# Hybrid backbone step on one core: eight modulation blocks move from the mixers to the attention, and the first two weight units are multiplied side by side

## The chip, the cores and the metric

The kernel is one launch on one core of a Trainium2 chip. The metric is device time in microseconds, the median of three runs. The core has five engines that run beside each other and meet at semaphores: TensorE (PE in the rows) for matrix products into PSUM, VectorE (DVE), ScalarE (ACT), GpSimd (POOL), and SyncE (SP), which here issues all the transfers between memory and SBUF. Each engine takes its instructions strictly in the order in which they are written, so an instruction that waits holds back everything behind it on its engine.

## What is computed

One layer of a diffusion backbone over 256 context tokens and 1024 latent tokens of width 1024. The part that matters here, cut from the reference:

```python
def _modulation(cond, w_mod, b_mod):
    m = jax.nn.silu(cond) @ w_mod + b_mod
    return jnp.split(m[:, None, :], N_MOD, axis=-1)      # six parts of 1024 values
...
    shift1, scale1, gate1, shift2, scale2, gate2 = mod
    h = _rmsnorm(x, norm1_g) * (1 + scale1) + shift1
    u = h @ w_in
    q, k, v, p_in, c_in, g_in = _split_in(u)
    y_a = ...attention(q, k, v)...  @ w_oa
    y_b = _pool_mixer(p_in, w_pool, pool_scale) @ w_ob
    y_c = _conv_mixer(c_in, w_dw, b_dw, conv_norm_g, conv_norm_b) @ w_oc
    gates = jax.nn.sigmoid(g_in + b_gate).reshape(B, L, N_BRANCH, D)
    x = x + gate1 * (merged @ w_out)
    h2 = _rmsnorm(x, norm2_g) * (1 + scale2) + shift2
    a, b = jnp.split(h2 @ w_gu, 2, axis=-1)
    x = x + gate2 * ((jax.nn.silu(a) * b) @ w_down)
```

`shift1` and `scale1` are needed at the very start. `gate1`, `shift2` and `scale2` (3072 columns of `w_mod`, 12 blocks of 256 columns, "late" in the kernel) are needed only after the attention, at the residual. There are two condition vectors, one for the latent tokens and one for the context.

## The kernel before

The program has three stages, each with one function per engine: front (`front_engines`, up to about 331 us), attention (`attention_engines`, to about 740 us) and rear (`rear_engines`). Every large product is done in three passes of a split operand, high by high, high by low and low by high (`products`, L143 to L148), so activations exist as `AH` and `AL` and weights as `w_hi` and `w_lo`.

**Front, first tiles.** The 1280 tokens are three chunks (512, 512 and 256 columns), the width is eight tiles of 128. VectorE and ScalarE make `AH` and `AL` tile by tile, in the order of `PAIRS`, eight tiles of chunk 0, eight of chunk 1, eight of chunk 2: `scaled` or the odd branch of `upper`, then `upper` writes `AH` (L677), then `rest` writes `AL` (L903). TensorE starts on weight units 0 and 1 while tiles still come. `unit_chunk(0, 0)` waits for each tile as it is made (L415 to L418); `unit_chunk(1, 0)` then goes over the same eight tiles again; then `spread_rstd(2)` (L538), whose result the normalisation of chunk 2 waits for; then units 0 and 1 on chunk 1, and on chunk 2, the first one waiting for tiles again. Products go to a ring of four PSUM banks (`RING`, `JOBS`): a bank is taken again when the job four before it has been read, by ScalarE or by VectorE (`glu_out`, L827).

**Front, the late modulation.** A block of 256 columns is loaded whole (1 MB, `load_mod`, L295), VectorE multiplies its eight row tiles by the two condition vectors into an accumulator (`modulation`, two instructions at L816 and fourteen at L819), and TensorE sums the accumulator over partitions with a column of ones (`modulation`, L431, four products written, eight in the records). All twelve blocks are made so, at the places of `MOD_AT` on TensorE and at the places written out in `vector`: six between 84 and 128 us, six between 259 and 317 us. Between them VectorE runs the 31 taps of the convolution (L839). `late_mod` adds the bias at the end of the front.

**Attention.** Eight heads of ten steps, 80 steps `s`, with `h = s // 10` and `n = s % 10`; steps 0 to 7 of a head are latent queries, 8 and 9 the context's. In step `s` TensorE does the scores of `s` (L1281 against the local keys, L1287 against the past ones), the transposes of step `s - 2` (L1296), and the products with V of step `s - 3` (L1310). Between them it does pieces of the gate projections (`gate_piece`, L147), spread evenly, which need nothing of the softmax. VectorE in its step `s` does: the maximum of the scores (`maximum`, L1440, L1443, L1445), the sum and reciprocal of `s - 1` (`total`, L1453, L1455), the sum of V products (`gather`, L1475), the low part of the transposed probabilities of `s - 2` (`lower`, L1462), and then in some steps more: `prepare` at `n == 5` (L1424) and `add_rows` at `n` 3 and 4 (L1481). ScalarE does the exponentials (L1361 past, L1364 local), the high part of the transposed probabilities (L1373), and between them gate rows (L1354) and splits of weights (L1333), keys (L1339), queries (L1342) and values (L1345). GpSimd normalises the probabilities (L1528), and makes the low parts of weights, keys and values and the bias tables (L1503, L1509, L1512, L1522).

The scores of step `s` use one pair of banks, so TensorE waits for ScalarE's exponential of the past scores of `s - 1` before it writes the next ones:

```python
                if s:
                    pe.wait_ge(past_ready, s)
```

and that exponential waits for VectorE's maximum of `s - 1`. This is the tightest tie between TensorE and VectorE in the stage.

**SyncE in the attention** walks the same steps: gate rows out, keys of the next head at `n == 0`, half of the position bias at `n` 1 and 2 (`load_b`, eight small transfers each, L1194), queries at 3, values at 6, weights between them (L1173).

## Time and profile before

| what | value |
|---|---|
| median of 3 runs | 1858.1 us (1857.86 to 1858.96) |
| the profiled execution: device time | 1857.35 us |
| the profiled execution: span of the instructions | 1855.5 us |
| TensorE busy | 1834.8 us, 99% |
| VectorE, ScalarE, GpSimd busy | 60%, 40%, 27% |
| granted clock of TensorE | 0.999 over the span |

The profile is one execution. Busy time is the union of an engine's instructions; TensorE's matmuls are pipelined, so they overlap in the records and the real cost of one is the distance from its start to the next one's start. A bracket behind a row tells how long the engine was idle before it and whose work ended that idle time. A row with no bracket followed at once on the one before it on its engine (gaps under about 0.15 us carry none).

### The profile page before, as it was taken

How to read it: one execution, taken by the hardware profiler on the slowest of the kernel's cores; microseconds unless marked ns; L12 is line 12 of the kernel's file. 1: busy time of each engine (PE TensorE's matmuls, PEld its weight loads, DVE VectorE, ACT ScalarE, POOL GpSimd, SP SyncE). 2: the span in 40 equal slices, each digit the busy share in tenths (PEclk: the TensorE clock that was granted, in tenths of full speed). 3: DMA queues.
4: the chain of work that ended last, by engine and by line, in shares of the span. 5: the costliest groups of instructions: out<-in, count | busy, mean ns of one | idle time of the engine just before them, and what ended most of it. 6: DMA issues, size and time to landing. Idle time of an engine off the chain costs nothing.

```text
span 1855.5 us, 26797 instructions
## 1 busy us (share of the span) xinstructions
PE 1834.8 (99%) x10034; PEld 1574.7 (85%) x10034; DVE 1115.5 (60%) x2090; ACT 748.4 (40%) x1412; POOL 500.5 (27%) x378
## 2 busy tenths in 40 slices
PE   8999999999999999999999999999999999999998
PEld 3788888898888888888888888888888888888898
DVE  4799997155655554276217755555444444799984
ACT  5612232355555554444224522222222223445474
POOL 0000000344444432144542243444434441000000
PEclk9999999999999999999999999999999999999999
DMA  8471345443344332765531222232122224866665
GB/s 329 160 225 48 113 130 190 114 133 104 101 111 113 104 99 67 240 186 173 189 125 46 97 69 91 97 97 67 54 74 74 74 74 169 280 210 222 210 215 199
DMA packets 221057, 253.91 MB, mean 137 GB/s; under 512 B 32384, under 2 KB 159872, under 8 KB 219904
## 3 DMA queue, kind: packets, MB, share of 16 engines
q1 hardware_dynamic: 220928, 252.20, 42.8%
q8 instruction: 80, 1.31, 0.3%
q14 instruction: 49, 0.40, 0.1%
HBM read 191.60 MB, written 60.56 MB: 136 GB/s over the span
## 4 chain that ended last, share of the span: by engine, by line
PE 95%; DVE 1%; DMA 1%; ACT 1%; issue 1%; POOL 0%; SPq 0%; ACTq 0%; DVEq 0%
PE ps_all L147 72%; PE ps_all L2425 5%; PE ps_all L2426 5%; PE ps_all L2427 4%; PE ps_all L1310 2%; PE ps_all L1296 2%; PE ps_all L1281 1%; PE ps_all L1287 1%; PE ps_all L527 1%; DMA wmod_block<-w_mod_dram 1%; PE ps_all L431 1%; DVE Y L3080 0%; PE ps_all L2459 0%; DMA wmod_then_mixers<-w_mod_dram 0%; PE ps_all L453 0%
## 5 line engine op out<-in xcount | busy, mean ns | idle before, releaser
L147 PE MATMUL ps_all<-AH,w_hi 128*128 128x512 f32 (+1 forms) x1376 | 493.4, 359 | 1.9 <-ACT gate_rows L1354 1.0
L147 PE MATMUL ps_all<-AH,w_lo 128*128 128x512 f32 (+1 forms) x1376 | 483.6, 351 | 0.0
L147 PE MATMUL ps_all<-AL,w_hi 128*128 128x512 f32 (+1 forms) x1376 | 483.1, 351 | 0.0
L147 PEld LDWEIGHTS ps_all<-AH,w_lo 128*128 128x128 f32 x1376 | 259.8, 189 | 35.9
L147 PEld LDWEIGHTS ps_all<-AH,w_hi 128*128 128x128 f32 x1376 | 260.2, 189 | 33.8 <-DVE AL L903 1.9
L147 PEld LDWEIGHTS ps_all<-AL,w_hi 128*128 128x128 f32 x1376 | 260.4, 189 | 30.3
L2999 DVE TENSOR_TENSOR quarter<-ps_all,quarter 128x512 f32<-128x512 f32 x140 | 96.6, 690 | 177.9 <-PE ps_all L147 175.8
L2852 POOL TENSOR_TENSOR slot_lo<-w_pair,slot_hi 128x512 fp32r<-128x512 f32 x96 | 129.8, 1376 | 174.1 <-ACT slot_hi L2623 174.1
L147 PE MATMUL ps_all<-AH,slot_hi 128*128 128x256 f32 (+1 forms) x384 | 129.5, 337 | 0.0
L147 PE MATMUL ps_all<-AL,slot_hi 128*128 128x256 f32 (+1 forms) x384 | 129.2, 336 | 0.0
L147 PE MATMUL ps_all<-AH,slot_lo 128*128 128x256 f32 (+1 forms) x384 | 129.1, 336 | 0.0
L2852 POOL TENSOR_TENSOR w_lo<-w_pair,w_hi 128x512 fp32r<-128x512 f32 x64 | 85.4, 1354 | 114.4 <-ACT w_hi L2623 114.4
L1462 DVE TENSOR_TENSOR PT<-ps_all,PT 128x256 fp32r<-128x256 f32 (+1 forms) x144 | 61.6, 465 | 83.6 <-ACT PT L1373 83.6
L1528 POOL TENSOR_SCALAR prob<-prob,softmax_cols 128x640 f32<-128x640 f32 (+2 forms) x80 | 57.5, 719 | 167.5 <-DVE softmax_cols L1455 167.2
L1361 ACT ACTIVATE prob<-ps_all,softmax_cols 128x256 f32<-128x256 f32 x80 | 38.0, 475 | 130.5 <-DVE softmax_cols L1445 113.5
L839 DVE SCALAR_TENSOR_TENSOR xT_then_mixers<-wmod_then_mixers,cols,xT_then_mixers 128x1295 f32<-128x1295 f32 x60 | 89.5, 1591 | 0.0
L2425 PE MATMUL ps_all<-AH 128*128 128x512 f32 (+1 forms) x248 | 86.9, 350 | 1.1 <-DVE AL L3035 1.1
L2427 PE MATMUL ps_all<-AH,AL 128*128 128x512 f32 (+1 forms) x248 | 86.3, 348 | 0.0
L2426 PE MATMUL ps_all<-AL,AH 128*128 128x512 f32 (+1 forms) x248 | 86.3, 348 | 0.0
L2425 PE MATMUL ps_all<-AH,w_hi 128*128 128x512 f32 (+1 forms) x236 | 83.9, 355 | 0.0
L2427 PE MATMUL ps_all<-AH,w_lo 128*128 128x512 f32 (+1 forms) x236 | 83.3, 353 | 0.0
L2426 PE MATMUL ps_all<-AL,w_hi 128*128 128x512 f32 (+1 forms) x236 | 83.3, 353 | 0.0
(307 smaller groups left out, 3948.8 us busy)
## 6 DMA issues: line engine op xcount, KB each, us to landing
w_raw<-w_in_dram SPq DMA_DIRECT2D x42, 512.0 KB
w_pair<-w_gu_dram SPq DMA_DIRECT2D x20, 1024.0 KB, 5.1
hidden_in<-hidden SPq DMA_DIRECT2D x77, 256.0 KB, 3.0
wmod_then_mixers<-w_mod_dram SPq DMA_DIRECT2D x19, 1024.0 KB, 8.1
hidden<-quarter SPq DMA_DIRECT2D x50, 256.0 KB, 2.1
branch_and_gates<-gates SPq DMA_DIRECT2D x16, 768.0 KB, 4.4
w_down_rows<-w_down_dram SPq DMA_DIRECT2D x44, 256.0 KB, 3.4
gates<-gate_rows SPq DMA_DIRECT2D x42, 256.0 KB, 2.2
```

What stands on the lines that cost most here:

```text
L147: mm = nc.tensor.matmul(out, w, a[:, k, cols[0]:cols[1]], start=(first and part == 0), stop=(last and part == 2))
L839: nc.vector.scalar_tensor_tensor(conv[:, t, :], glu[:, t, k:k + CV], w, conv[:, t, :], ALU.mult, ALU.add).then_inc(conv_step, 1)
L1296: mm = nc.tensor.transpose(psT[:, turned_at(j):turned_at(j) + P], prob[:, s % 3, j * P:(j + 1) * P], g.ident[:, :])
L1310: mm = nc.tensor.matmul(psV[s % 2][:, 0:2 * P], VV[:, b, v, :], PT[:, s % 2, j, :], start=(m == 0), stop=(m == len(both) - 1))
L1361: nc.scalar.activation(pr[:, LOCAL:PCOLS], psS_past, ACT.Exp, bias=c[:, 2:3], accum_out=c[:, 4:5]).then_inc(past_ready, 1)
L1462: nc.vector.tensor_tensor(PT[:, s % 2, j0:j1, P:2 * P], psT[:, turned_at(j0):turned_at(j0) + (j1 - j0) * P].rearrange("p (j n) -> p j n", ...
L1528: nc.gpsimd.tensor_scalar(pr[:, a:PCOLS], pr[:, a:PCOLS], c[:, 5:6], 1.0, ALU.mult, ALU.mult).then_inc(normal, 1)
L2425: nc.tensor.matmul(out, wh, th, start=first, stop=False)
L2426: nc.tensor.matmul(out, wh, tl, start=False, stop=False)
L2427: return nc.tensor.matmul(out, wl, th, start=False, stop=last)
L2852: nc.gpsimd.tensor_tensor(tiles4(lo), in_pair(p, idx), tiles4(hi.bitcast(F32)), ALU.subtract).then_inc(s_lo, 1)
L2999: nc.vector.tensor_tensor(temp[TEMP[out][side]][:, :], g.ps_all[:, product_bank(p, source), :], temp[TEMP[first][side]][:, :], ALU.add).th ...
```

## The change

Two edits.

1. Four of the twelve late blocks stay in the front, at new places of `MOD_AT`. The other eight are made in the attention, one per head: SyncE loads 1 MB into a single buffer `late_wmod` at step `n == 1`, VectorE does the sixteen instructions in groups of 2, 2, 2, 2, 3, 3, 2 at the ends of its steps `n` = 3 to 9 (`MOD_OPS`), and TensorE sums them at step `n == 2` of the next head. The copy from PSUM and `late_mod` move to the end of the attention. The semaphores of the modulation become shared over the stages, and the rear's `gate2` counts on from them.
2. Units 0 and 1 are multiplied side by side in `first_units`, so that each tile is used by both units when it comes; in chunk 1 the first four tiles are still taken by unit 0 alone and then by unit 1 alone, the last four by both.

```diff
-MOD_AT = {(2, 2): (0,), (3, 0): (1,), (3, 1): (2,), (4, 0): (3,), (4, 1): (4,), (5, 0): (5,), (13, 2): (6,),
-          (14, 0): (7,), (15, 0): (8,), (15, 1): (9,), (16, 1): (10,), (17, 0): (11,)}
+MOD_STEPS = 2 * KD
+MOD_ALL, MOD_FRONT = 3 * D // (2 * P), 4
+MOD_AT = {(3, 0): (0,), (3, 2): (1,), (4, 1): (2,), (5, 0): (3,)}
+MOD_OPS = {3: (0, 2), 4: (2, 4), 5: (4, 6), 6: (6, 8), 7: (8, 11), 8: (11, 14), 9: (14, 16)}
...
+            def first_units(c):
+
+                a, b = CHUNKS[c]
+                pe.wait_ge(W.lo_ready, 2)
+                out = {}
+                alone = 4 if c == 1 else 0
+                for k, units in [(k, (u,)) for u in range(2) for k in range(alone)] + [(k, (0, 1)) for k in range(alone, KD)]:
+                    w = slice(k * P, (k + 1) * P)
+                    pe.wait_ge(ah_ready, c * KD + k + 1)
+                    for u in units:
+                        if k == 0:
+                            out[u] = bank(JOB["unit", u, c])[:, 0:b - a]
+                        hi, lo = w_slot(u)
+                        nc.tensor.matmul(out[u], hi[:, w], g.AH[:, k, a:b], start=(k == 0), stop=False)
+                        nc.tensor.matmul(out[u], lo[:, w], g.AH[:, k, a:b], start=False, stop=False)
+                    pe.wait_ge(al_ready, c * KD + k + 1)
+                    for u in units:
+                        mm = nc.tensor.matmul(out[u], w_slot(u)[0][:, w], g.AL[:, k, a:b], start=False, stop=(k == KD - 1))
...
-            unit_chunk(0, 0)
-            unit_chunk(1, 0)
+            first_units(0)
             spread_rstd(2)
-            for c in (1, 2):
-                for u in range(2):
-                    unit_chunk(u, c)
+            first_units(1)
+            first_units(2)
...
             lower(4)
-            modulation(3)
-            modulation(4)
             for c in range(3):
                 glu_out(1, c)
             lower(5)
-            modulation(5)
+            modulation(3)
...
             lower(14)
-            modulation(6)
-            modulation(7)
             normalise()
-            lower(15)
-            modulation(8)
-            modulation(9)
-            lower(16)
-            modulation(10)
-            lower(17)
-            modulation(11)
-            lower(18)
-            late_mod()
+            for u in range(15, 19):
+                lower(u)
...
+            def load_mod(n):
+                if n > MOD_FRONT:
+                    sp.wait_ge(acc_step, MOD_STEPS * n)
+                sp.dma_start(late_w[:, :, :], g.d["w_mod"].rearrange("(k p) n -> p k n", p=P)[:, :, 2 * D + n * 2 * P:2 * D + (n + 1) * 2 * P]).then_inc(mod_in, 16)
...
+                if n == 1 and h < MOD_ALL - MOD_FRONT:
+                    load_mod(MOD_FRONT + h)
...
+                if s % QT == 2 and s > QT:
+                    pe.wait_ge(summed_v, s - TIMES - 1)
+                    modulation(MOD_FRONT + s // QT - 1)
...
+            def modulation(n, first, last):
+                if first == 0:
+                    dve.wait_ge(mod_in, 16 * (MOD_FRONT // 2 + n - MOD_FRONT + 1))
+                    dve.wait_ge(mod_used, n)
+                for at in range(first, last):
+                    k, j = at // 2, at % 2
+                    w, c, acc = late_w[:, k, :], g.cs[:, at:at + 1], late_acc[:, j, :]
+                    if k == 0:
+                        nc.vector.tensor_scalar(acc, w, c, None, ALU.mult).then_inc(acc_step, 1)
+                    else:
+                        dve.wait_ge(acc_step, MOD_STEPS * n + at - 1)
+                        nc.vector.scalar_tensor_tensor(acc, w, c, acc, ALU.mult, ALU.add).then_inc(acc_step, 1)
...
+                if n in MOD_OPS and h < MOD_ALL - MOD_FRONT:
+                    modulation(MOD_FRONT + h, *MOD_OPS[n])
             add_rows(HEADS - 1, 1)
+            late_mod()
```

TensorE, units 0 and 1 on chunk 0. Before, unit 0's last tile and then the start of unit 1 over the same tiles:

```order
L415 MATMUL ps_all<-AH,w_hi 128x512 [waits ah_ready]
L416 MATMUL ps_all<-AH,w_lo 128x512
L418 MATMUL ps_all<-AL,w_hi 128x512 [waits al_ready]
L147 MATMUL ps_all<-AH,w_hi 128x512 [waits w_lo_ready]
L147 MATMUL ps_all<-AL,w_hi 128x512
L147 MATMUL ps_all<-AH,w_lo 128x512
```

After, one tile:

```order
L425 MATMUL ps_all<-AH,w_hi 128x512 [waits ah_ready]
L426 MATMUL ps_all<-AH,w_lo 128x512
L425 MATMUL ps_all<-AH,w_hi 128x512
L426 MATMUL ps_all<-AH,w_lo 128x512
L429 MATMUL ps_all<-AL,w_hi 128x512 [waits al_ready]
L429 MATMUL ps_all<-AL,w_hi 128x512
```

Each wait for a tile has six products behind it in place of three, and the pass of unit 1 over chunk 0 that waited for nothing is gone.

VectorE, the end of step 4 of head 0 and the start of step 5 in the attention. Before:

```order
L1475 TENSOR_REDUCE OT<-ps_all 128x16x8 [waits times_v]
L1462 TENSOR_TENSOR PT<-ps_all,PT 128x3x128 [waits p_hi0]
L1462 TENSOR_TENSOR PT<-ps_all,PT 128x2x128 [waits p_hi1]
L1440 ISA prob,softmax_cols<-ps_all,bias 128x384 [waits t_done1,local_scored]
L1443 TENSOR_REDUCE softmax_cols<-ps_all 128x1 [waits scored]
```

After, from the end of step 3 of the same head to the same place:

```order
L1498 TENSOR_SCALAR late_mod_acc<-late_wmod,silu_c 128x256 [waits mod_acc_used,late_wmod_in0]
L1498 TENSOR_SCALAR late_mod_acc<-late_wmod,silu_c 128x256
L1447 ISA prob,softmax_cols<-ps_all,bias 128x384 [waits t_done1,local_scored]
...
L1469 TENSOR_TENSOR PT<-ps_all,PT 128x3x128 [waits p_hi0]
L1469 TENSOR_TENSOR PT<-ps_all,PT 128x2x128 [waits p_hi1]
L1501 SCALAR_TENSOR_TENSOR late_mod_acc<-late_wmod,silu_c,late_mod_acc 128x256 [waits mod_acc_step] x2
L1447 ISA prob,softmax_cols<-ps_all,bias 128x384 [waits t_done1,local_scored]
```

The new instructions stand between the low part of one step and the maximum of the next; the first of a head waits for the block's transfer.

SyncE, step 1 of head 0. Before:

```order
L1179 DMA kq_src<-kT_dram 64x1536 [waits v_lo]
L1179 DMA kq_src<-kT_dram 64x1536
L1194 DMA bias_src<-rpb_dram 8x8x24 [waits bias_ready]
L1194 DMA bias_src<-rpb_dram 8x8x24 x7
L1207 DMA gates<-gate_rows 128x512 [waits gate_free]
```

After:

```order
L1166 DMA kq_src<-kT_dram 64x1536 [waits v_lo]
L1166 DMA kq_src<-kT_dram 64x1536
L1181 DMA bias_src<-rpb_dram 8x8x24 [waits bias_ready]
L1181 DMA bias_src<-rpb_dram 8x8x24 x7
L1204 DMA late_wmod<-w_mod_dram 128x8x256
L1194 DMA gates<-gate_rows 128x512 [waits gate_free]
```

The block's load stands behind the keys and the first half of the bias, and ahead of the next gate rows.

## Rows read from the trace of the kernel before

**Rows 1.** Table by stretch, the attention (columns: stretch, its length, busy per engine, clock).

```profile
350.00:740.00 390.00, 388.98 (x2376) 345.43 (x2375) 213.74 (x662) 217.49 (x551) 158.34 (x130) 1.00 0.38 104
```

**Rows 2.** The chain that ended last, in order of time: start us, us, what.

```profile
165.25 5.46 PE ps_all L147 x24
170.93 8.35 PE ps_all L147 x48
```

**Rows 3.** TensorE in order of time, first units: start us, us, engine, line, instruction.

```profile
49.56 0.47 PE L415 MATMUL ps_all<-AH,w_hi 128*128 128x512 f32 x1 [1.03 <-ACT AH L677]
...
59.18 0.50 PE L418 MATMUL ps_all<-AL,w_hi 128*128 128x512 f32 x1 [0.70 <-DVE AL L903]
...
71.39 0.50 PE L147 MATMUL ps_all<-AH,w_hi 128*128 128x512 f32 x1 [0.62 <-DVE AL L903]
...
83.41 1.04 PE L482 MATMUL ps_all<-ident,vt 128*128 128x128 f32 x8
```

**Rows 4.** VectorE in order of time beside them: tiles of AL, and the first `glu_out`.

```profile
64.15 0.69 DVE L903 TENSOR_TENSOR AL<-normed,AH 128x512 fp32r<-128x512 f32 x1
...
70.65 0.69 DVE L903 TENSOR_TENSOR AL<-normed,AH 128x512 fp32r<-128x512 f32 x1
...
74.70 0.68 DVE L827 TENSOR_TENSOR wmod_then_mixers<-ps_all,sig 128x512 f32<-128x512 f32 x1
```

**Rows 5.** TensorE in order of time, one block of the late modulation and what follows.

```profile
98.07 0.95 PE L431 MATMUL ps_all<-ones,mod_acc 128*128 128x1 f32 x8
98.88 0.48 PE L147 MATMUL ps_all<-AH,w_hi 128*128 128x512 f32 x1
```

**Rows 6.** VectorE, one block of the late modulation, in order of time.

```profile
83.95 0.61 DVE L816 TENSOR_SCALAR mod_acc<-wmod_then_mixers,silu_c 128x256 f32<-128x256 f32 x2
84.48 5.63 DVE L819 SCALAR_TENSOR_TENSOR mod_acc<-wmod_then_mixers,silu_c,mod_acc 128x256 f32<-128x256 f32 x14
```

**Rows 7.** View of the buffer `wmod_then_mixers`, 80 to 340 us: its transfers' landing.

```profile
DMA to landing us min/median/max: 5.1/7.0/10.1
```

**Rows 8.** Waits in the attention: who, for whom, us in total, times, longest.

```profile
DVE prob L1440 <- PE ps_all L1281: 52.1, 37, 4.0
```

**Rows 9.** VectorE, head 1: start of the maximum in steps 5 to 7.

```profile
428.21 0.54 DVE L1440 CUSTOM_DVE_ANT_0 prob<-ps_all,bias 128x384 f32<-128x384 f32 x1
...
433.91 0.56 DVE L1440 CUSTOM_DVE_ANT_0 prob<-ps_all,bias 128x384 f32<-128x384 f32 x1
...
437.48 0.42 DVE L1440 CUSTOM_DVE_ANT_0 prob<-ps_all,bias 128x256 f32<-128x256 f32 x1
```

**Rows 10.** ScalarE, then TensorE: head 1, past scores of step 6 read, step 7 written.

```profile
435.10 0.47 ACT L1361 ACTIVATE prob<-ps_all,softmax_cols 128x256 f32<-128x256 f32 x1 [2.74 <-DVE softmax_cols L1445]
...
436.88 0.28 PE L1287 MATMUL ps_all<-KA,QS 128*128 128x256 f32 x1
```

**Rows 11.** The same two in head 5, steps 6 and 7.

```profile
621.19 0.48 ACT L1361 ACTIVATE prob<-ps_all,softmax_cols 128x256 f32<-128x256 f32 x1 [2.53 <-DVE softmax_cols L1445]
...
622.00 0.28 PE L1287 MATMUL ps_all<-KA,QS 128*128 128x256 f32 x1
```

**Rows 12.** GpSimd, then VectorE, in head 1: the low keys and a one-column sum.

```profile
413.59 3.51 POOL L1509 TENSOR_TENSOR KB<-kq_src,KA 128x1536 fp32r<-128x1536 f32 x1 [1.87 <-ACT KA L1339]
...
414.75 2.36 DVE L1453 TENSOR_TENSOR softmax_cols<-softmax_cols 128x1 f32<-128x1 f32 x1
```

**Rows 13.** VectorE by shape, 1060 to 1300 us: one addition, two sources (xcount, busy, mean ns).

```profile
L3012 DVE SCALAR_TENSOR_TENSOR quarter<-quarter,quarter 128x512 f32<-128x512 f32 x17 | 19.0, 1136 | 1.0
...
L3012 DVE SCALAR_TENSOR_TENSOR quarter<-ps_all,quarter 128x512 f32<-128x512 f32 x4 | 2.7, 681 | 0.0
```

**Rows 14.** SyncE, VectorE and TensorE in head 0, steps 1 to 5.

```profile
370.75 2.93 SPq L1194 DMA_DIRECT2D bias_src<-rpb_dram  x8
...
375.88 0.55 DVE L1440 CUSTOM_DVE_ANT_0 prob<-ps_all,bias 128x384 f32<-128x384 f32 x1
...
380.32 0.28 PE L1287 MATMUL ps_all<-KA,QS 128*128 128x256 f32 x1
```

More of the change, by code:

```diff
@@ L412, in unit_chunk @@
                     w = slice(k * P, (k + 1) * P)
-                    if u == 0 and c == 0:
-                        pe.wait_ge(ah_ready, k + 1)
-                        nc.tensor.matmul(out[:, 0:b - a], hi[:, w], g.AH[:, k, a:b], start=(k == 0), stop=False)
-                        nc.tensor.matmul(out[:, 0:b - a], lo[:, w], g.AH[:, k, a:b], start=False, stop=False)
-                        pe.wait_ge(al_ready, k + 1)
-                        mm = nc.tensor.matmul(out[:, 0:b - a], hi[:, w], g.AL[:, k, a:b], start=False, stop=(k == KD - 1))
-                        continue
-                    if u == 0:
-                        pe.wait_ge(al_ready, c * KD + k + 1)
                     mm = products(nc, out[:, 0:b - a], hi[:, w], lo[:, w], g.AH, g.AL, k, (a, b), k == 0, k == KD - 1)
                 mm.then_inc(done, 1)
+            def first_units(c):
[15 more added lines that the diff above has]
+                        mm = nc.tensor.matmul(out[u], w_slot(u)[0][:, w], g.AL[:, k, a:b], start=False, stop=(k == KD - 1))
+                        if k == KD - 1:
+                            mm.then_inc(done, 1)
             def modulation(n):
@@ L1023, in gpsimd @@
             nc.gpsimd.tensor_tensor(sig[:, :], sig[:, :], square, ALU.add).then_inc(sq_summed, 1)
-        return Engines(sync, tensor, scalar, vector, gpsimd, ((mod_step, 2), (branch_stored, 16 * 6)), after, signals)
+        return Engines(sync, tensor, scalar, vector, gpsimd, ((W.lo_ready, MIX + 1), (branch_stored, 16 * 6)), after, signals)
 V_PARTS = ((0, 4), (4, 8), (8, 10))
@@ L1121, in attention_engines @@
         st = sb("softmax_cols", [P, 4, 6])
+        late_w = nc.alloc_sbuf_tensor_at("late_wmod", [P, KD, 2 * P], F32, offset=aligned(nc.sbuf_base))
+        late_acc = nc.alloc_sbuf_tensor_at("late_mod_acc", [P, 2, 2 * P], F32, offset=aligned(nc.sbuf_base) + 4 * KD * 2 * P)
+        mod_in, acc_step, mod_used, mod_out, mod_step = g.mod_in[0], g.acc_step, g.mod_used, g.mod_out, g.mod_step
         psG = g.ps_all[:, 0:2, :]
@@ L1311, in value, with modulation @@
                 mm.then_inc(times_v, 1)
+            def modulation(n):
+                pe.wait_ge(acc_step, MOD_STEPS * (n + 1))
+                for m in range(2):
+                    for j in range(2):
+                        c = 4 * n + 2 * m + j
+                        mm = nc.tensor.matmul(g.modp[:, c:c + 1], late_acc[:, j, m * P:(m + 1) * P], g.ones[:, 0:1], start=True, stop=True)
+                mm.then_inc(mod_used, 1)
             for x in range(LEAD):
@@ L1481, in add_rows, with late_mod @@
                 nc.vector.tensor_tensor(rows, rows, OLO[:, 0:b - a], ALU.add).then_inc(out_ready, 1)
+            def modulation(n, first, last):
[10 more added lines that the diff above has]
+                        nc.vector.scalar_tensor_tensor(acc, w, c, acc, ALU.mult, ALU.add).then_inc(acc_step, 1)
+            def late_mod():
+                dve.wait_ge(mod_out, 1)
+                mod = g.mod[:, 2 * KD:5 * KD, :]
+                nc.vector.tensor_tensor(mod, mod, g.cols[:, OFF["b_mod"] + 2 * KD:OFF["b_mod"] + 5 * KD].rearrange("p (m j) -> p m j", j=1).broadcast_to([P, 3 * KD, 2]),
+                                        ALU.add).then_inc(mod_step, 1)
+                dve.wait_ge(mod_step, 1)
+                mod_gain(g, 1, "norm2_g", 4, mod_step)
             prepare(0)
```

57 lines of the change are left out of this document (24 added, 33 removed).

## The prediction

> **What bounds the kernel now.** I read four views, in this order. The table by stretch first: over the attention TensorE is busy 389.0 of 390 us, VectorE 213.7, GpSimd 158.3 [rows 1]. So the time is TensorE's work plus the few places where it stands, and whatever is put on VectorE is free just as long as TensorE does not come to wait for it. The chain gives the price of that work: 24 products of 512 columns take 5.46 us, 0.2275 us each, and 24 of 512 with 24 of 256 take 8.35 us, so one of 256 costs 0.120 us [rows 2]. TensorE's own timeline then shows where it stands: from the first product of unit 0 at 49.56 us to the transposes of the cached keys at 83.41 us it needed 33.85 us [rows 3] for 96 products of 512 columns (21.84 us) and 48 of 256 (5.76 us), 27.6 us in all. About 6.2 us of this stretch is waiting for tiles, and TensorE has no other such hole. Last, the waits inside the attention, to see how far VectorE is from being late there.
>
> **Part 1, the first units.** Nothing is added or removed, only the order changes. The walk, with tiles counted 1 to 24 over the three chunks. Chunk 0: both units take 1.365 us per tile; the last AL tile of the chunk comes at 59.1 (the product that waited for it starts at 59.18 [rows 3]), the pace of TensorE is slower than that of the tiles, so it runs 48 products without standing, 49.56 + 10.92 = 60.5. Before, unit 1 ended at about 65.0. Chunk 1: unit 0 alone meets tile 12, whose AL ends at 64.15 + 0.69 = 64.84 [rows 4], so its fourth tile is done at 65.1; unit 1 alone takes 2.73, to 67.9; the last four tiles for both take 5.46, to 73.3, the last tile being there since 71.34 [rows 4]. Before, both ended at about 77.7. Chunk 2: unit 1's bank is free only when VectorE has read job (1, 0), an instruction at 74.70 that ends at 75.38 [rows 4] and stands behind tile work in VectorE's order; since the spread for chunk 2 comes earlier, it may move up by 0.6. TensorE gets the bank at about 74.9 and needs 0.24 less than 5.76 from there: 80.4. Against 83.41 that is **3.0 us gained**, half of the hole. The other half is held by the making of tiles and by that bank. It can't be more than 6.2 (no hole left) or less than 0 unless the later bank wait grows by 3 us, for which no row speaks.
>
> **Part 2, the eight blocks leave the front.** On TensorE one block costs 98.88 - 98.07 = 0.81 us [rows 5]. Eight are taken out of the front and eight put into the attention: 0 in the sum. On VectorE one block costs 0.53 for its first two instructions and 5.63 for the other fourteen, 0.40 each [rows 6], 6.1 us together. Taking them out of the front buys nothing by itself, since TensorE waits for no VectorE work between 85 and 331 us; it gives cover, so that VectorE keeps ahead of a TensorE that now comes 3 us sooner. The transfers are the same eight megabytes.
>
> **Part 3, the eight blocks in the attention.** Of the 64 maxima of the latent steps only 37 waited for TensorE's scores [rows 8]; the other 27 started when VectorE had finished its previous step. In those steps VectorE and ScalarE are one serial chain: maximum, exponential, high part, low part, then rows or queries, then the next maximum. In head 1 the maxima of steps 5, 6 and 7 start at 428.21, 433.91 and 437.48 with no idle time before them [rows 9]. The new instructions stand exactly there, between low part and maximum, so each is added whole to the chain. TensorE notices when ScalarE's exponential of the past scores comes too late. In head 1 that of step 6 ends at 435.57 and TensorE's next past scores start at 436.88 [rows 10], their weight load about 0.1 before, so 1.2 us are to spare; the delay by then is 0.6 + 0.8 + 0.8 = 2.2 us, less the 0.8 by which TensorE's own block at step 2 puts it later. In head 5 the same pair stands at 621.67 and 622.00 [rows 11], 0.2 to spare, and 1.65 arrives. I carried the delay from step to step through all heads in this way, adding 0.6, 0.8, 0.8, 0.8, 1.2, 1.2 and 0.8 at steps 3 to 9, taking off what VectorE idled before a maximum, and counting what goes beyond the room before each step's past scores: 0.0, 0.6, 0.3, 0.7, 0.3, 1.4, 0.0 and 1.1 us for heads 0 to 7, **4.5 us lost**. If the delay is a fifth smaller, the same walk gives about 1.4, if a fifth larger, about 8.
>
> To this come two things that the count of instructions doesn't have. **The port.** While GpSimd ran the low keys from 413.59 to 417.10, VectorE's one-column addition of 0.15 us, started at 414.75, ended at 417.11 [rows 12]. Of the 64 such additions ten took over 0.3 us, and each of the ten ended within 0.03 us of a GpSimd instruction with two sources in SBUF. Fourteen of a block's sixteen instructions read two sources in SBUF, and GpSimd does its weights, tables and values in steps 6 to 8, after VectorE's sum of the same step, so they meet. In the rear an addition with both sources in SBUF took 1136 ns mean beside GpSimd, 681 ns with one source in PSUM [rows 13], 1.67 times. By that ratio the ten instructions of steps 6 to 9 cost 4.0 x 0.67 = 2.7 us more per head, 21 us in all; some is taken up by VectorE's idle time in steps 9 to 2. Ends: 0 if they never meet, and 22 by the same walk if every meeting that today's order shows is paid in full. I take a third, **7.5 us**. The Trainium skill states the mechanism (SBUF — State Buffer, Who interferes with whom): a VectorE instruction with two SBUF inputs and a GpSimd instruction that reads SBUF block each other for the whole instruction, whichever starts first. The trace agrees with it in the ten cases; taken for every meeting it would make the sum some 14 us larger than mine, which is the upper end above.
>
> **The transfer in head 0.** SyncE's last bias transfer of step 1 is issued by 373.68, the block's load right behind it; the maximum of step 4, before which VectorE now takes the block's first two instructions, started at 375.88 [rows 14]. The same load landed in 5.1, 7.0 and 10.1 us (least, median, most) in the front [rows 7], so it comes at 378.8 to 383.8. VectorE stands for 3 to 8 us. TensorE's past scores of step 5 at 380.32 [rows 14] have 2.6 us of room, and the chain of steps 5 to 7 is full. With a wait of 4.2 the walk gives 4.1 us, with 3 it gives 2.9, with 8 it gives 7.9. I take **4 us**. In the other heads step 3 comes some 10 us after the load's issue, and it is there.
>
> **The sum.** -3.0 + 4.5 + 7.5 + 4.0 = +13.0 us. On the profiled execution's 1857.35 that is 1870.4; it lies 0.75 under the median, so on the median it is 1871.1. The end of the attention (copy and bias, below 1 us on ScalarE and VectorE) is hidden: both stand idle for over 5 us there, and the bank that waits for the copy is the last of eight.
>
> **The rivals.**
> *Covered.* VectorE has 176 us idle in the attention [rows 1] and the 49 us fit in. TensorE never waits beyond a microsecond or two, and the 3.0 stay: 1855.1, up to 1858 with part of head 0's wait. For it speaks that no PE wait on VectorE shows in the stage; against it rows 9 to 11, where room is 0.2 and 1.2 us.
> *Faster, by the whole hole.* The tiles of chunk 1 and 2 come sooner than in my walk, since TensorE's earlier spread frees VectorE and the bank read moves up, and all 6.2 us go: 1858.1 - 6.2 = 1851.9, if the attention is covered too. It decides whether AL's 16th tile is made before about 70. Against it: VectorE shows no idle time between 56 and 65 us.
> *Transfers.* The megabyte per head also delays weights and gate rows that are queued behind it, and ScalarE stands for them in order. In head 5 weights are issued right behind it. It adds 1 to 5 us per head where it hits: 1885 and over.
>
> **How the numbers follow.** Chances: the forecast (VectorE's chain gets too long in the attention, port and first transfer with it) 0.62, own range 1862 to 1885; covered 0.2; the whole hole 0.08; transfers 0.1. The most likely time is that of the forecast, 1871. The range reaches down to the covered case, 1855, and up to 1886, where head 0 waits the longest and the port costs double. A measurement of this kernel can tell about 0.2%, 3.7 us, from no change. Faster by more than that: the whole hole and a little of the covered case, 0.13. Within it: most of the covered case and the mildest end of the forecast, 0.22. Slower: 0.65.
>
> **What would show it.** Right: TensorE reaches the cached keys' transposes 2.5 to 3.5 us earlier; the front ends about 9.5 us earlier; in the attention TensorE waits at the scores (now L1270 to L1281) for ScalarE, most in head 0 and in steps 6 to 9; the attention is longer by 6.5 us of products plus 10 to 22 us of standing; the new products' partner on VectorE, L1501, has a mean over 0.5 us with single ones over 1 us; L1498 waits for `late_wmod` in head 0. Wrong: VectorE's steps 3 to 7 keep their length, which would mean that the chain had room that I took for none; or L1501 keeps 0.48 us throughout, and the port term is 0; or the first block's load lands before 376.

## The result

The changed kernel takes 1872.24 us (median, 1871.31 to 1872.58) against 1857.86 (1857.66 to 1858.96): ratio 1.0075, 95% interval 1.0066 to 1.0085. The prediction was 1871.1, slower. Its profiled execution has a span of 1870.3 us, 14.8 more than before.

The span, cut at TensorE's own marks (its first product of unit 0, the transposes of the cached keys, the first scores, the last product with V), says where:

| stretch | before | after | difference | predicted |
|---|---|---|---|---|
| start to first product | 49.56 | 49.78 | +0.2 | 0 |
| first units | 33.85 | 30.82 | -3.0 | -3.0 |
| rest of the front | 275.18 | 267.54 | -7.6 | -6.5 |
| attention | 380.61 | 406.34 | +25.7 | +22.5 |
| rear | 1116.3 | 1115.8 | -0.5 | 0 |

Of the attention's 25.7, 7.2 are the eight blocks' products. The prediction took 0.81 a block [rows 5], but the first product behind a block also starts its successor 0.09 late, so a block is 0.90, here as in the front, and moving it cancels. The other 18.5 are time in which TensorE stands or runs at half clock; 16.0 had been predicted.

The table by stretch of the changed kernel, the attention, answers to [rows 1] (stretch, length, busy per engine, clock):

```profile
350.00:740.00 390.00, 380.13 (x2294) 334.73 (x2293) 275.69 (x774) 205.05 (x535) 153.79 (x126) 0.99 0.44 119
```

TensorE is now busy 380.1 of 390, and VectorE 275.7 instead of 213.7. That is 62 us more in a stretch where 49 had been counted. VectorE still stands idle for 114 us here, and the work costs TensorE 18 us all the same.

The first units, in order of time, answer to [rows 3] and [rows 4] (start us, us, engine, line, instruction, in brackets the idle time and who ended it):

```profile
49.78 0.47 PE L425 MATMUL ps_all<-AH,w_hi 128*128 128x512 f32 x1 [1.02 <-ACT AH L683]
...
73.74 0.28 PE L426 MATMUL ps_all<-AH,w_lo 128*128 128x256 f32 x1
74.98 0.39 PE L425 MATMUL ps_all<-AH,w_hi 128*128 128x256 f32 x1 [0.97 <-DVE wmod_then_mixers L830]
...
80.60 1.04 PE L490 MATMUL ps_all<-ident,vt 128*128 128x128 f32 x8
```

49.78 to 80.60 is 30.82; the last wait is for the bank that `glu_out` reads, as the walk had it: 74.98 and 80.60 against 74.9 and 80.4.

The groups of instructions over the attention (xcount, busy us, mean ns, idle before) and two waits (who, for whom, us in total, times, longest):

```profile
L1501 DVE SCALAR_TENSOR_TENSOR late_mod_acc<-late_wmod,silu_c,late_mod_acc 128x256 f32<-128x256 f32 x112 | 69.9, 670 | 0.1
...
L1498 DVE TENSOR_SCALAR late_mod_acc<-late_wmod,silu_c 128x256 f32<-128x256 f32 x16 | 5.9, 409 | 4.4 <-DMA late_wmod<-w_mod_dram 4.4
```

```profile
PE ps_all L1281 <- ACT prob L1366: 5.8, 9, 1.4
...
PE ps_all L1275 <- DVE softmax_cols L1447: 2.4, 1, 2.4
```

The accumulations have a mean of 0.67 us. The view of their tile gives the least as 0.469, the middle as 0.477 and the longest as 2.619: most are as short as in the front, and 22 of 112 took 0.6 to 2.6. Each of the 22 started while a GpSimd instruction ran and ends 0.27 to 0.28 us behind its end. Nine of the 90 short ones overlap one too; there it was GpSimd that started later. The costliest piece in head 2:

```profile
488.71 3.41 DVE L1501 SCALAR_TENSOR_TENSOR late_mod_acc<-late_wmod,silu_c,late_mod_acc 128x256 f32<-128x256 f32 x3
489.18 2.66 POOL L1534 TENSOR_TENSOR w_lo<-w_raw,w_hi 128x1024 fp32r<-128x1024 f32 x1 [1.61 <-ACT w_hi L1338]
```

Three accumulations take 3.41 us instead of 1.2, since the third ends only when GpSimd's low part of the weights has ended at 491.84.

The last large piece is head 0. TensorE in order of time (rows between are left out where the dots stand), then the table by stretch beside it (the eighth column, behind GpSimd's, is the granted clock):

```profile
368.93 0.75 PE L1304 MATMUL ps_all<-PT,VV 128*128 128x256 f32 x5
372.11 0.69 PE L1275 MATMUL ps_all<-KA,QS 128*128 128x384 f32 x1 [2.43 <-DVE softmax_cols L1447]
...
374.31 0.63 PE L149 MATMUL ps_all<-AL,w_hi 128*128 128x512 f32 x1
374.74 0.63 PE L149 MATMUL ps_all<-AH,w_lo 128*128 128x512 f32 x1
```

```profile
366.00:369.00 3.00, 3.00 (x19) 2.62 (x19) 0.00 (x0) 1.49 (x1) 1.30 (x1) 1.00 1.06 353
...
374.00:376.00 2.00, 2.00 (x6) 1.53 (x6) 1.75 (x5) 0.85 (x3) 0.00 (x0) 0.50 0.74 193
...
378.00:380.00 2.00, 2.00 (x9) 1.60 (x8) 0.89 (x2) 2.00 (x6) 0.27 (x2) 0.79 0.01 4
```

VectorE stood 4.4 us for the first block's load (the eight loads land, by the view of their buffer, 5.2 to 6.0 us after the issue), TensorE 2.4 for VectorE. Not all of this is the load. VectorE's first two instructions behind it, and GpSimd beside them:

```profile
369.87 1.70 DVE L1498 TENSOR_SCALAR late_mod_acc<-late_wmod,silu_c 128x256 f32<-128x256 f32 x2 [4.37 <-DMA late_wmod<-w_mod_dram]
367.70 3.46 POOL L1540 TENSOR_TENSOR KB<-kq_src,KA 128x1536 fp32r<-128x1536 f32 x1 [3.59 <-ACT KA L1344]
```

The two take 1.70 us instead of the 0.61 of [rows 6]: the late load put the first of them beside GpSimd's low keys, and 1.1 us of the wait are this meeting. When TensorE went on, a product of 512 columns took 0.43 us instead of 0.23, until 378.9: the granted clock was 0.50, that is 1.2 GHz. The 6.7 us at half clock did the work of 3.4, so 3.3 us were lost on top of the 2.4. No step of the prediction had that.

### The profile page after: what moved, and what is told of

The parts are those of the page before. It is cut to its first block, busy times and chain, and to the rows that moved or that the text cites. A ratio compares the mean times of both kernels' runs of the same rounds, so it can differ in the third digit from the quotient of the medians.

```text
span 1870.3 us, 26800 instructions
## 1 busy us (share of the span) xinstructions
PE 1841.1 (98%) x10034; PEld 1579.4 (84%) x10034; DVE 1136.1 (61%) x2090; ACT 745.3 (40%) x1412; POOL 502.9 (27%) x378
## 4 chain that ended last, share of the span: by engine, by line
PE 83%; DVE 6%; ACT 4%; issue 3%; DMA 2%; POOL 1%; SPq 0%; ACTq 0%; DVEq 0%; POOLq 0%
PE ps_all L149 63%; PE ps_all L2457 4%; PE ps_all L2459 4%; PE ps_all L2458 4%; DVE late_mod_acc L1501 2%; PE ps_all L1304 1%; PE ps_all L1290 1%; ACT PT L1378 1%; PE ps_all L535 1%; DMA wmod_block<-w_mod_dram 1%; DVE prob L1447 1%; ACT prob L1369 1%; DVE PT L1469 1%; PE ps_all L1281 1%; PE ps_all L1275 1%
## 5 line engine op out<-in xcount | busy, mean ns | idle before, releaser
L149 PE MATMUL ps_all<-AH,w_hi 128*128 128x512 f32 (+1 forms) x1336 | 479.5, 359 | 0.7 <-ACT gate_rows L1359 0.5
L149 PE MATMUL ps_all<-AH,w_lo 128*128 128x512 f32 (+1 forms) x1336 | 470.3, 352 | 0.0
L149 PE MATMUL ps_all<-AL,w_hi 128*128 128x512 f32 (+1 forms) x1336 | 470.0, 352 | 0.0
L149 PEld LDWEIGHTS ps_all<-AH,w_lo 128*128 128x128 f32 x1336 | 252.7, 189 | 35.0
L149 PEld LDWEIGHTS ps_all<-AH,w_hi 128*128 128x128 f32 x1336 | 253.2, 190 | 31.1 <-ACT gate_rows L1359 1.0
L149 PEld LDWEIGHTS ps_all<-AL,w_hi 128*128 128x128 f32 x1336 | 253.3, 190 | 29.7
L2457 PE MATMUL ps_all<-AH,w_hi 128*128 128x512 f32 (+1 forms) x236 | 83.9, 355 | 0.0
L2459 PE MATMUL ps_all<-AH,w_lo 128*128 128x512 f32 (+1 forms) x236 | 83.3, 353 | 0.0
L2458 PE MATMUL ps_all<-AL,w_hi 128*128 128x512 f32 (+1 forms) x236 | 83.3, 353 | 0.0
```

What stands on the lines that cost most here:

```text
L149: mm = nc.tensor.matmul(out, w, a[:, k, cols[0]:cols[1]], start=(first and part == 0), stop=(last and part == 2))
L2457: nc.tensor.matmul(out, wh, th, start=first, stop=False)
L2458: nc.tensor.matmul(out, wh, tl, start=False, stop=False)
L2459: return nc.tensor.matmul(out, wl, th, start=False, stop=last)
```

## The experiments

The walk through the attention had three terms: the chain's length 4.5, the port 7.5, the first load 4.0. The accounts to be told apart were that transfers do it, that the port (GpSimd holding up VectorE) costs nothing on the path, and that the two parts of the change are independent of each other. The times of the kernel before beside these runs were 1858.0 to 1858.5 us (median).

**1. The first units alone** (the kernel before with `first_units`):

```diff
-            unit_chunk(0, 0)
-            unit_chunk(1, 0)
+            first_units(0)
             spread_rstd(2)
-            for c in (1, 2):
-                for u in range(2):
-                    unit_chunk(u, c)
+            first_units(1)
+            first_units(2)
```

> The kernel before with the new order of the first two units and nothing else; all twelve blocks stay beside the mixers. My theory, that the two parts are independent: TensorE is 3.0 us earlier at the transposes of the cached keys and keeps it to the end, 1857.9 - 3.0 = 1854.9. Rival, that the gain needs the blocks out of the front (VectorE must keep ahead of a TensorE that comes sooner): the 3.0 us are given back by waits before 331 us, 1857.9.

**2. The blocks alone** (the changed kernel with those lines as before):

> The changed kernel with the first two units in the old order. If the parts are independent, it loses the 3.0 us and stands at 1872.2 + 3.0 = 1875.2. If the new order only moved waits about, it stands at 1872.2.

Measured: alone, the first units bring nothing, 1858.86 us, ratio 1.0001 (0.9991 to 1.0010). The blocks alone take 1875.0 (1.009, 1.0075 to 1.0105), 2.8 over the changed kernel. So the new order is worth 2.8 with four blocks in the front and nothing with twelve. In run 1 TensorE was at the transposes after 30.83 us, as in the changed kernel, and lost the gain again from 118.8 us on. VectorE and TensorE there, and the table by stretch:

```profile
114.93 5.62 DVE L829 SCALAR_TENSOR_TENSOR mod_acc<-wmod_then_mixers,silu_c,mod_acc 128x256 f32<-128x256 f32 x14
...
120.48 1.61 DVE L837 TENSOR_TENSOR wmod_then_mixers<-ps_all,sig 128x512 f32<-128x512 f32 x3
...
121.21 0.80 PE L147 MATMUL ps_all<-AH,w_hi 128*128 128x512 f32 x1 [2.38 <-DVE wmod_then_mixers L837]
```

```profile
121.00:124.30 3.30, 3.09 (x7) 2.48 (x8) 3.30 (x8) 0.00 (x0) 0.00 (x0) 0.50 0.80 247
```

TensorE waits for a bank that `glu_out` has to read, and `glu_out` stands behind the fourteen accumulations of block 4. Again it stands 2.4 us, and again the clock is at half behind it, to 124.4. The kernel before came to this place at 121.0 us, when the read that it needs, begun at 119.7, was done, and had neither.

**3. The first load before step 0, and 5, in step 0.** The block is loaded ahead of the loop of steps, or behind the weights of unit 3:

```diff
             load_v(0)
+            load_mod(MOD_FRONT)          # run 3
             for s in range(STEPS_END + 1):
...
                 if s == 0:
                     load_w(3)
+                    load_mod(MOD_FRONT)  # run 5
...
-                if n == 1 and h < MOD_ALL - MOD_FRONT:
+                if n == 1 and 0 < h < MOD_ALL - MOD_FRONT:
```

> The changed kernel with one transfer moved: the first block of the attention is loaded before step 0 instead of in step 1. In the changed kernel head 0 is longer than before by 5.65 us beyond its block's 0.81, the others by 1.1 to 2.8, 1.9 in the mean. My theory: VectorE's wait for the load holds up TensorE, which stands and is then granted half its clock for some 6.7 us; both go, 3.8 us, 1868.4, and no stretch of half clock is left. Rival, the half clock has nothing to do with the wait: the clock falls all the same, and about half of the 3.8 stays, 1870.3.

Measured: 1871.29 (1.0071, 1.0056 to 1.0086), a miss. The half clock is gone and head 0 is 1.4 us shorter, not 3.8. ScalarE's row in head 0 says why:

```profile
357.50 1.06 ACT L1339 ACTIVATE w_hi<-w_raw 128x1024 fp32r<-128x1024 f32 x1 [4.60 <-DMA w_raw<-w_in_dram]
```

The megabyte now ran ahead of the weights of unit 3, ScalarE stood 4.6 us for those, with the exponentials behind it in its order. This is the prediction's transfer rival, made by the experiment and not by the change.

> The changed kernel with the first block's load in step 0 right behind the weights of unit 3 (before step 0 it pushed those weights back and ScalarE stood 4.6 us for them). My theory, that head 0 lost 3.8 us to the wait for the load and to the half clock that followed it: head 0 goes from 51.5 to 47.8 us and the kernel to 1868.4. Rival, whatever place the megabyte has, it pushes some other transfer back, and head 0 stays at about 50: 1871.

Measured: 1868.94 (1.0055, 1.0040 to 1.0070), head 0 is 48.04 us instead of 51.53, the attention 402.56 instead of 406.34. The first load's place is worth 3.8 us of the attention (3.3 by the two medians, which were taken beside different runs of the kernel before). Runs 6, 7, 9 and 10 build on this one.

**4. One source instead of two** (on run 3; the adding up is left out):

```diff
-                        nc.vector.scalar_tensor_tensor(acc, w, c, acc, ALU.mult, ALU.add).then_inc(acc_step, 1)
+                        at0 = min(k * 2 * P, KD * 2 * P - ONE_WIDE)
+                        nc.vector.tensor_scalar(acc, late_w.ap().rearrange("p k n -> p (k n)")[:, at0:at0 + ONE_WIDE], c, None, ALU.mult).then_inc(acc_step, 1)
```

> As the run before, and the fourteen accumulations of a block in the attention are replaced by products with one source in SBUF, of 314 columns instead of 256 so that one takes the same 0.40 us; the adding up is left out, so the modulation of those columns is not computed. Same count, same place, same time of one. If the shared port is what made 22 of the 112 take 0.64 to 2.6 us, none of them does now, VectorE's share is 45 us instead of 70, and only my term for the lengthened chain is left: 1854.9 + 4.5 = 1859.4. Rival, the long ones cost nothing on the path and the chain's own length is what TensorE waits for: 1868.

Measured: 1864.62 (1.0034, 1.0021 to 1.0047), between the two. It does not test what it was made for. The view of the tile:

```profile
L1504 DVE TENSOR_SCALAR late_mod_acc<-late_wmod,silu_c x112: 366/376/2512, 372.5 to 734.3; 128x314 f32<-128x314 f32 x112
```

25 of the 112 are long again, up to 2.5 us. And they were not of equal length: from start to start one took 0.29 us, not 0.40. The gain of 6.7 us over run 3 is put down to the shorter instructions, which this run doesn't show by itself; what it does show is that one source in SBUF does not avoid GpSimd.

**6 and 10. Reductions** (on run 5), over 384 and over 320 columns:

```diff
-                        nc.vector.scalar_tensor_tensor(acc, w, c, acc, ALU.mult, ALU.add).then_inc(acc_step, 1)
+                        at0 = min(k * 2 * P, KD * 2 * P - ONE_WIDE)
+                        nc.vector.tensor_reduce(acc[:, at:at + 1], late_w.ap().rearrange("p k n -> p (k n)")[:, at0:at0 + ONE_WIDE], AX, ALU.add).then_inc(acc_step, 1)
```

> As the run before, and each of the fourteen accumulations is replaced by a reduction over 384 columns of the same block: one source in SBUF, one column written, an estimated 0.40 us each. The modulation of these columns is left out. In the run with products of one source 24 of 112 were still long, so the number of sources does not decide. Theory A, any VectorE instruction with a source in SBUF meets GpSimd: again some 20 long ones, VectorE's share about 70 us, and the kernel at 1868. Theory B, the reduction does not take the port: no long ones, share 45 us, and the standing in heads 1 to 7 falls to my chain term, 1860.

> The reductions again over 320 columns instead of 384. With 384 one took 0.46 us from start to start, not the 0.40 of an accumulation; with 320 it should take 0.39. So this is the chain's length at the right size with no meeting. By the walk of the prediction, 4.5 us at this length, on the 1854.5 of the run that keeps two of sixteen: 1859.0. Rival, the standing does not fall so steeply with the length: over 1861.

Measured: 1863.19 with 384 columns (1.0026, 1.0016 to 1.0035) and 1860.49 with 320 (1.0015, 1.0005 to 1.0025). No reduction is long. The view of the tile with 320, and then the same place in head 1, step 6, first of the changed kernel, then with reductions:

```profile
L1504 DVE TENSOR_REDUCE late_mod_acc<-late_wmod x112: 466/475/488, 370.5 to 730.2; 128x1 f32<-128x320 f32 x112
```

```profile
434.58 2.38 POOL L1534 TENSOR_TENSOR w_lo<-w_raw,w_hi 128x1024 fp32r<-128x1024 f32 x1
...
435.88 1.76 DVE L1501 SCALAR_TENSOR_TENSOR late_mod_acc<-late_wmod,silu_c,late_mod_acc 128x256 f32<-128x256 f32 x2
```

```profile
430.24 2.38 POOL L1537 TENSOR_TENSOR w_lo<-w_raw,w_hi 128x1024 fp32r<-128x1024 f32 x1
...
431.53 0.87 DVE L1504 TENSOR_REDUCE late_mod_acc<-late_wmod 128x1 f32<-128x320 f32 x2
```

GpSimd runs the same instruction over the same moment; two accumulations take 1.76 us, two reductions 0.87, which is their time alone. With 320 columns a reduction is as long as an accumulation alone (middle 0.475 and 0.477), in the same count and place. So this pair, runs 5 and 10, differs by the meetings only: attention 402.56 and 393.87, **8.7 us**. Theory B of run 6 holds. The tables by stretch of run 5, run 10 and, for what follows, run 7 (TensorE's busy time is the first number behind the length, VectorE's the third):

```profile
350.00:735.00 385.00, 376.40 (x2286) 331.35 (x2286) 272.89 (x770) 205.37 (x534) 154.08 (x125) 1.00 0.44 120
...
350.00:735.00 385.00, 381.92 (x2332) 337.95 (x2331) 254.50 (x782) 209.60 (x541) 154.86 (x128) 1.00 0.44 121
...
350.00:735.00 385.00, 384.65 (x2371) 342.52 (x2370) 213.41 (x672) 211.90 (x543) 154.95 (x128) 1.00 0.45 124
```

The meetings are 18 us of VectorE's time, and TensorE loses about half of that.

**7. Two of sixteen** (on run 5):

```diff
-                for at in range(first, last):
+                for at in range(first, min(last, 2)):
...
-                        nc.vector.tensor_scalar(acc, w, c, None, ALU.mult).then_inc(acc_step, 1)
+                        nc.vector.tensor_scalar(acc, w, c, None, ALU.mult).then_inc(acc_step, MOD_STEPS // 2)
```

> As the load in step 0, with only the first two of a block's sixteen instructions left on VectorE (fourteen left out, so the modulation of these columns is not computed); all loads and all of TensorE's products stay. My theory, that transfers cost nothing by themselves in heads 1 to 7: attention as long as before plus 8 x 0.9 for the products, 380.6 + 7.2 = 387.8, and the kernel at 1855 to 1856. Rival, the loads hold up weights and gate rows: 1 us or more per head, 1862 or over.

Measured: 1854.47 (0.9979, 0.9969 to 0.9988), attention 388.26, 0.5 over before plus the products, all of it in head 0. Eight megabytes and eight blocks of products cost nothing more; the transfer rival is out for heads 1 to 7. From here to run 10 only VectorE's work grows, by 41 us (254.50 against 213.41): 393.87 - 388.26 = **5.6 us**, the chain's length by itself.

**9. Ahead of the low part** (on run 5): the call of `modulation` is moved in front of `lower(s - TURN)`.

```diff
+                if n in MOD_OPS and h < MOD_ALL - MOD_FRONT:
+                    modulation(MOD_FRONT + h, *MOD_OPS[n])
                 if 0 <= s - TURN < STEPS:
                     lower(s - TURN)
...
-                if n in MOD_OPS and h < MOD_ALL - MOD_FRONT:
-                    modulation(MOD_FRONT + h, *MOD_OPS[n])
```

> As the load in step 0 (1868.9), and in a step the block's instructions stand ahead of VectorE's low part of the probabilities instead of behind it. There VectorE waits for ScalarE's high part, 69 us in 74 waits, 0.93 each, and two instructions take 0.8. Theory, the price is the place in the chain: the part that is only length (with reductions, which never meet GpSimd, 8 of the 14 us of standing) goes, what the meetings cost stays: 1861. Rival, the chain is a sum wherever the instructions stand: 1868.9.

Measured: 1865.25 (1.0039, 1.0024 to 1.0054), attention 399.35: 3.2 us better, not 8. The view of the tile and a wait:

```profile
L1502 DVE SCALAR_TENSOR_TENSOR late_mod_acc<-late_wmod,silu_c,late_mod_acc x112: 468/827/2627, 368.2 to 733.4; 128x256 f32<-128x256 f32 x112
```

```profile
PE ps_all L1291 <- DVE PT L1470: 6.5, 7, 1.6
```

In the new place the accumulations meet GpSimd's normalising of the probabilities: 70 of 112 are long, 45 of these end just behind a normalising, and the middle one of all takes 0.83 us. TensorE now stands for the low part that comes behind them. The gap in VectorE's order was real, but it is the gap in which GpSimd works.

**8, 11 and 12. All twelve blocks in the front, with the new order of the first units.** In run 8 the products of the second gate unit stand ahead of block 4:

```diff
             modulation(3)
-            modulation(4)
             for c in range(3):
                 glu_out(1, c)
+            modulation(4)
             lower(5)
```

> The kernel before with the new order of the first units, and in VectorE's order the three products of the second gate unit (L827) stand ahead of block 4 instead of behind it; all twelve blocks in the front. In the run with the first units alone TensorE stood 2.4 us at 118.6 for the first of these three, which waited behind block 4, and was then granted half its clock to 124.4; that ate the gain. If that is all, the 3.0 us come through: 1855.4. If the next wait in line takes its place: 1858.

Measured: 1856.64 (0.9989, 0.9980 to 0.9998). The stand at 118.8 is gone, and 1.8 of the 3.0 arrive, against the 1858.45 of the kernel before beside it (the 1.3 in what was expected of run 11 counts from 1857.9). The waits of the front name the next in line:

```profile
PEld ps_all L147 <- DVE w_lo L815: 1.3, 2, 1.0
PEld ps_all L147 <- ACT gate_rows L1364: 1.3, 1, 1.3
```

They are the low parts of weights that VectorE makes between the taps of the convolution, at 200 and 216 us, and gate rows at 353.

Run 11 takes block 5 behind the convolution as well, and the bias to the end of the attention; run 12 also puts a low part between any two of the last three. VectorE's order, run 8 against run 12 (in run 11 blocks 9 and 10 stand together ahead of `lower(17)`; the places on TensorE and of the loads, which follow this order and are the same in runs 11 and 12, are left out):

```diff
             lower(5)
-            modulation(5)
...
             lower(14)
+            modulation(5)
             modulation(6)
-            modulation(7)
             normalise()
             lower(15)
+            modulation(7)
             modulation(8)
-            modulation(9)
             lower(16)
-            modulation(10)
+            modulation(9)
             lower(17)
-            modulation(11)
+            modulation(10)
             lower(18)
+            modulation(11)
-            late_mod()
```

> All twelve blocks in the front again, new order of the first units, the second gate unit's products ahead of block 4, and block 5 moved from before the convolution to behind it (seven late blocks instead of six); the bias of the modulation is added at the end of the attention. VectorE enters the convolution 6 us sooner. With the gate products first the kernel was at 1856.6: 1.3 of the 3.0 us came through, since TensorE then waited 0.3 and 0.9 us at 200 and 216 us for the low parts of weights which VectorE makes between taps. Theory, VectorE is the second limit of the front and this gives it room: 1855.2. Rival, the longer late part holds TensorE up between 265 and 330 us: 1857 or over.

> As the run with seven late blocks, but behind the convolution every block stands between two low parts of weights on VectorE (block 9, low part of unit 17, block 10, low part of unit 18, block 11); the attention's first transfers wait for the last block. With blocks 9 and 10 in one piece TensorE stood 3.7 us at 311 for the low part of unit 17 and 1.9 at 358.8 for gate rows, whose place in ScalarE's order is behind keys that came 4.5 us later. Theory, VectorE's order is all that stood in the way, the whole 3.0 us come through: 1855.2, or 1855.6 with a little of the end. Rival, the second limit of the front is VectorE's total work and another low part comes late: 1857 or over.

Measured: run 11 takes 1862.43 (1.0023, 1.0013 to 1.0033), run 12 takes 1854.33 (0.9980, 0.9971 to 0.9989), faster than both kernels of this study. In run 11 most is one wait of TensorE, for a low part behind two blocks, with half clock to 318 behind it:

```profile
PE ps_all L150 <- DVE w_lo L809: 3.7, 1, 3.7
```

A second stand, 1.9 us at 356.9 for gate rows, has half clock behind it too. Run 12 has no wait of TensorE for VectorE between 82 us and the attention, and its VectorE does the same work there, so the amount of work was not the limit. That VectorE's order alone is worth the 8.1 us between runs 11 and 12 is not shown: run 12 also lets the attention's first transfers go at the last block instead of the last low part, and which of the two removed the stand for gate rows is open.

## Why the prediction came out right, and where it did not

**First units, -3.0:** measured -3.03. The walk over tiles, and the bank behind job (1, 0), hold to 0.2 us. But runs 1 and 2 show that this term was not the property of the edit: with twelve blocks in the front and VectorE's order as it was, it is worth nothing. The sentence that TensorE waits for no VectorE work between 85 and 331 us was read from the old trace and holds for the old TensorE. Part 2 named the cover that the moved blocks give and priced it at nothing; beside the old order of VectorE it is the whole 3.0, and run 12 shows that the cover can be had without moving a block, by another order.

**Chain, 4.5:** measured 5.6 (runs 7 and 10). The walk from step to step, with 0.2 to 3 us of room before each step's past scores [rows 10, 11], is good to a fifth in the sum. (The eight numbers that it lists add up to 4.4.) By head it is less good, and part of the agreement is luck: it gave 0.0, 0.6, 0.3, 0.7, 0.3, 1.4, 0.0 and 1.1 us for heads 0 to 7, and run 10 is longer than run 7 by 1.0, 1.5, 0.3, 0.7, 1.0, 1.1, 0.0 and 0.0. The walk also had the steepness: with instructions a sixth longer (run 6) the attention is 3.8 us longer, but 2.0 of these are in head 0, where TensorE stood 1.4 for ScalarE, which had itself waited 4.4 us for weights; 1.8 are in the other heads. VectorE has over 100 us idle at the same time; by the share of busy time, the covered rival, it should have cost nothing.

**Port, 7.5:** measured 8.7 (runs 5 and 10), inside 0 to 22. That it came near the third that I had taken is luck: the prediction had rows for the two ends and none for the third. The ratio under it was misread as well: of the 17 additions of [rows 13] five ran beside no GpSimd instruction and took 0.69, the other twelve took 1.0 to 1.8. The reason given was also incomplete. The count of sources does not decide: products with one source met GpSimd as often (run 4), reductions with one source never (runs 6, 10). The Trainium skill has what I had left out (SBUF — State Buffer, Who interferes with whom): not only an instruction with two SBUF inputs but also one that runs in a 2-port performance mode takes the shared pair, and VectorE: DVE Perf Modes, What auto-detection actually checks, says that a single source and a destination both in SBUF choose such a mode, where their outermost dimensions are even or equal. The 256 and 314 columns here are even. The runs agree: from start to start 58 columns more cost a product 0.030 us (256 columns in 0.262, 314 in 0.292), while 64 columns more cost a reduction 0.067 (320 in 0.393, 384 in 0.460), so a column more costs the product half as much, and only the product met GpSimd.

**First transfer, 4.0:** measured 3.8 (run 5), right in size for half a reason, and in part by luck. The load landed 6.0 us after its issue, and VectorE stood 4.4. The walk had 4.2, for which the prediction gives no row: its own median landing of 7.0 gives 380.7, 4.8 us behind 375.88. What TensorE then lost was 2.4 of standing, in which the meeting with the low keys has 1.1, and some 3.3 of half clock, 5.7 together. Run 5, without them, gets back 3.5 in head 0, so 2.2 are lost there in another way; its first two accumulations now take 2.56 us instead of 0.8 beside the same low keys. The walk took all of it for standing.

**The sum** was 13.0 and the profiled spans differ by 14.8: chain 1.1 and port 1.2 more than forecast, 0.5 left in run 7, the rear and the start -0.3, the rest of the front -0.4 beyond the blocks, the first transfer -0.2. The terms were missed in both directions by little. "The front ends about 9.5 us earlier" was 10.5, most of the difference from the price of a block.

**The rivals.** *Covered* is excluded: run 10 against run 7 shows a loss already without any meeting. *The whole hole* is excluded: the first units took 30.82 us, and 27.6 would be without any waiting. *Transfers* is excluded for heads 1 to 7 by run 7; run 3 shows that in head 0 a load in another place does hold up weights.

## What to carry to other kernels

Before work is moved onto an engine with idle time, find the chain through it, walk its slack step by step, and ask what the neighbouring engine does in the gap that is to be filled: here part of VectorE's idle time was where GpSimd worked, and an instruction that met it was held until GpSimd's had ended. A gain of a few us upstream has to be followed to the next wait of the engine that now comes earlier; the order of the work there, such as one block between two low parts, can be worth all of it. Place a large transfer by what is queued behind it, not only by when it is needed.

## What the hardware showed that was not expected

Once the products of the first units had begun, every stand of TensorE between 1.9 and 3.7 us, up to the end of the attention, was followed by a granted clock of 0.50 (1.2 GHz): 2.4 us in the changed kernel and in run 1, 2.3 in run 2, 3.7 and 1.9 in run 11. In the changed kernel TensorE worked 6.7 us under it, in run 1 some 3.2. None of the shorter stands in that part was, the longest being 1.6 us in run 9 and 1.4 in the changed kernel. In the changed kernel the wait thus cost more than double.

The length of the stand alone does not decide it. Before the first units a stand of 2.1 us at 29 us in run 3 had the full clock behind it. And the stand of 1.0 us just ahead of the first units, which every kernel here has, was followed by half clock in runs 5, 7, 9 and 12 and by the full clock in the others:

```profile
50.09 0.77 PE L425 MATMUL ps_all<-AH,w_hi 128*128 128x512 f32 x1 [1.02 <-ACT AH L683]
...
50.00:53.30 3.30, 3.21 (x8) 2.57 (x9) 2.94 (x6) 3.24 (x6) 0.00 (x0) 0.50 1.07 362
```

That is run 5, TensorE and the table by stretch. It cost nothing there: the first units took 30.8 us in these runs as in the changed kernel, since they wait for tiles and a bank. What decides it is open.

A VectorE accumulation that meets GpSimd does not slow down by a ratio. When GpSimd had started first, it is held until GpSimd's instruction has ended and then takes a time that goes with its own width: the 22 long ones of 256 columns end 0.27 to 0.28 us behind it, the twelve additions of 512 columns in the rear of the kernel before 0.55, and the ten one-column ones of the kernel before 0.01 to 0.02. What they met in the changed kernel was the low part of weights (5 times, 2.4 to 2.7 us long), the low part of V (7, 1.9 to 2.0), the bias tables (7, 1.0 to 1.2) and the normalising (3, 0.7 to 0.9). The ratio of 1.67 from the rear [rows 13] is a mean over such cases and over additions that met nothing.
